# An expert mixer on one Trainium2 core: gathers of four experts for each of 32 tokens, V sums in four column strips, token copies by way of DRAM

## The reference

```python
s = jnp.einsum('nhcd,hckd->nhck', q, keys)
s1, i1 = lax.top_k(s[:, :, 0], PEER_TOPK)
s2, i2 = lax.top_k(s[:, :, 1], PEER_TOPK)
top, sel = lax.top_k(cand, PEER_TOPK)
eidx = jnp.take_along_axis(cidx, sel, axis=-1)
gate = jax.nn.softmax(top, axis=-1)
hid = gelu(jnp.einsum('nkd,nd->nk', U[eb], xb))
out = jnp.einsum('nk,nkd->nd', hid * gb, V[eb])
```

## Time and profile before

| | us |
|---|---|
| median of 3 runs (lowest, highest) | 2206.36 (2205.28, 2214.78) |
| the profiled execution, its own time | 2209.18 |
| its span, first to last instruction | 2207.1 |
| TensorE busy | 2025.8 (92%) |
| VectorE busy | 1443.1 (65%) |
| ScalarE busy | 857.4 (39%) |
| GpSimd busy | 747.4 (34%) |

### The profile page before, as it was taken

The page is one execution under the profiler, slowest core; times in us unless marked ns, Lnnn a source line. Parts: engine busy times, 40 slices in busy tenths (PEclk is TensorE's granted clock), DMA queues, the critical chain, the costliest instruction groups (busy, mean ns, idle before and its releaser), DMA issues.

```text
span 2207.1 us, 37965 instructions
## 1 busy us (share of the span) xinstructions
PE 2025.8 (92%) x13044; PEld 1241.8 (56%) x13044; DVE 1443.1 (65%) x3377; ACT 857.4 (39%) x2476; POOL 747.4 (34%) x658
## 2 busy tenths in 40 slices
PE   7999989999999888999899898899999998789997
PEld 6777668874444223554478776788644442234544
DVE  2425454589999998545442344645999989975555
ACT  2221222144545775433332203221544557753332
POOL 0400000025545676544312000000345557765552
PEclk9999989999999999999999998999999999999999
DMA  6330233678999999999843201437699999999995
GB/s 278 116 116 2 81 112 128 213 254 315 321 352 359 374 354 355 365 379 391 325 187 116 95 8 74 145 134 260 230 325 335 362 370 365 373 380 389 373 383 233
DMA packets 121546, 569.81 MB, mean 258 GB/s; under 512 B 42504, under 2 KB 44712, under 8 KB 61608
## 3 DMA queue, kind: packets, MB, share of 16 engines
q0 software_dynamic: 76032, 389.07, 46.9%
q1 hardware_dynamic: 43648, 175.12, 21.7%
q10 hardware_dynamic: 1696, 3.45, 0.4%
HBM read 725.63 MB, written 6.58 MB: 332 GB/s over the span
## 4 chain that ended last, share of the span: by engine, by line
PE 58%; DVE 21%; issue 10%; DMA 5%; ACT 5%; POOL 1%; another core or an unknown queue 0%; DVEq 0%; SPq 0%; ACTq 0%; POOLq 0%
PE ps L1088 12%; PE ps L1007 11%; PE ps L607 10%; PE ps L672 7%; DVE arena L2091 5%; PE ps L929 3%; PE ps L962 3%; PE ps L943 3%; DMA arena<-in_uv,arena 3%; DMA ring<-in_uv,arena 2%; PE ps L1036 2%; DVE arena L1986 1%; DVE arena L2116 1%; DVE arena L1977 1%; DVE arena L1976 1%
## 5 line engine op out<-in xcount | busy, mean ns | idle before, releaser
L1524 POOL DMA_INDIRECT arena<-in_uv,arena x264 | 342.9, 1299 | 281.3 <-PE ps L1007 229.7
L1524 POOL DMA_INDIRECT ring<-in_uv,arena x264 | 317.8, 1204 | 256.0 <-PE ps L1007 208.6
L2091 DVE SCALAR_TENSOR_TENSOR arena<-arena 128x1024 bf16<-128x1024 f32 x264 | 319.9, 1225 | 118.8 <-DMA arena<-in_uv,arena 113.7
L2091 DVE SCALAR_TENSOR_TENSOR arena<-ring,arena 128x1024 bf16<-128x1024 f32 x264 | 320.3, 1225 | 110.0 <-DMA ring<-in_uv,arena 103.3
L1007 PE MATMUL ps<-arena 64*64 64x512 f32 x2112 | 292.6, 626 | 50.3 <-ACT arena L1416 50.1
L1007 PE MATMUL ps<-ring,arena 64*64 64x512 f32 x2112 | 286.7, 614 | 37.4 <-ACT arena L1416 35.0
L1414 ACT ACTIVATE arena<-arena 128x1 f32<-128x1 f32 x528 | 105.7, 200 | 506.7 <-DVE arena L2091 505.6
L1514 POOL COPY arena<-arena 128x8 uint32 (+1 forms) x66 | 36.4, 552 | 734.9 <-DVEq L2058 734.5
L1088 PEld LDWEIGHTS ps<-hold,ub 128*128 128x128 f32 x1024 | 180.4, 190 | 159.9 <-issue 142.8
L1088 PE MATMUL ps<-hold,ub 128*128 128x256 f32 x1024 | 268.2, 397 | 0.0
L672 PE MATMUL ps<-xn,ring 128*128 128x264 f32 x1024 | 244.5, 398 | 14.3 <-remote 12.2
(11 more groups left out here) (453 smaller groups left out, 2475.9 us busy)
## 6 DMA issues: line engine op xcount, KB each, us to landing
ring<-in_w SPq DMA_DIRECT2D x84, 1024.0 KB, 5.0
ub<-in_uv SPq DMA_DIRECT2D x64, 512.0 KB, 7.7
ub<-in_ud SPq DMA_DIRECT2D x48, 512.0 KB, 7.5
hold<-in_ud SPq DMA_DIRECT2D x16, 512.0 KB, 6.1
ring<-in_uv,arena POOLq DMA_INDIRECT x264, 8.5
arena<-in_uv,arena POOLq DMA_INDIRECT x264, 9.3
ub<-in_w SPq DMA_DIRECT2D x4, 1024.0 KB, 11.0
hold<-in_st SPq DMA_DIRECT2D x2, 2048.0 KB
```

Of the source, the lines that this page charges most:

```text
L1524: e.indirect_dma_start(out=row(k), out_offset=None, in_=A["uv"], in_offset=bass.IndirectOffsetOnAxis(ap=ix[:, par, k:k + 1], axis=0), **sk ...
L2091: stt(prod[:, n % 2, :], u, 1.0, xtok[:, tt, :], ALU.mult, ALU.mult, accum_out=hid[:, k:k + 1]).then_inc(S("dve_hid"), 1)
```

## The change

A gather now serves 32 tokens with four experts each: partition 32 q + t holds expert q of a group's token t. A tile is four groups g; for each two heads (r) and each group there are eight gathers, so their number stays the same. `place(s)` gives tile, r and g of a slot. VectorE multiplies with `rep`, a copy of a group's 32 tokens on all four quarters of the partitions. SyncE makes it: it writes `xtok` to DRAM and reads each group back with the row block named four times (`copies_of_rows`); the reads of the second tile wait until the first tile's last dots of that group are done. The diagonal is 128x32 (`token`), and the sum takes four matmuls over all 128 rows, each with 32 columns of the array and 256 channels of V.

Indices and gates, which routing writes per token, are moved into the new order by ScalarE (`by_tokens`, four copies of 32 partitions for each r and g) into `lay`, and GpSimd waits for these copies (`act_lay`) in place of the routing signal, which comes after the gates. `rep` and `lay` lie over constants that the expert mixer doesn't use; after layer 0 ScalarE loads them again. The first half of the second tile's sum (its groups 0 and 1) is copied, turned and added before the samples' sum is complete, and the second half alone is left for the end. Some loops on TensorE and GpSimd become straight code. Some semaphores are joined (`sp_svw` and `sp_svr`, `dve_yy`, `dve_yc` and `dve_yn`), without another order.

```diff
+TG = 32
+QS = P // TG
...
+    t["group"] = (p[:, None] // 16 == np.arange(TG)[None]).astype(float)
+    t["token"] = (p[:, None] % TG == np.arange(TG)[None]).astype(float)
...
+OVER = CONST_AT["headsum"][0]
...
-        eidx = carve(TT, SLOTS)
-        gate_w = carve(TT, SLOTS)
+        eg = carve(TT, 2, SLOTS)
...
+        rep = const[:, OVER:OVER + QS * D].rearrange("p (a b) -> p a b", b=D)
+        lay = const[:, OVER + QS * D:OVER + QS * D + TT * 2 * SLOTS].rearrange("p (a b) -> p a b", b=2 * SLOTS)
...
-        dg = carve(SLOT, HD)
+        dg = carve(SLOT, TG)
...
+        def place(s):
+
+            tt, n = divmod(s, P)
+            return tt, n // (QS * SLOT), n // SLOT % QS
+
+        def at_place(s):
+
+            tt, r, g = place(s)
+            return (r * QS + g) * 2 * SLOT
...
+                def copies_of_rows(tt):
+
+                    e.wait_ge(S("act_xt"), tt + 1)
+                    e.dma_start(O["scratch_x"][tt * P:tt * P + P, :], xtok[:, tt, :]).then_inc(S("sp_rep"), 16)
+                    for g in range(QS):
+                        if tt:
+                            e.wait_ge(S("dve_hid"), P - (QS - 1 - g) * SLOT)
+                        e.wait_ge(S("sp_rep"), 16 * ((QS + 1) * tt + g + 1))
+                        src = O["scratch_x"][tt * P + g * TG:tt * P + g * TG + TG, :]
+                        e.dma_start(rep[:, g, :], bc(src, 0, [QS, TG, D])).then_inc(S("sp_rep"), 16)
+
...
+                        if j == AHEAD[-1] + 2:
+                            copies_of_rows(0)
...
-                down_blocks(0, 12)
+                down_blocks(0, UB)
+                copies_of_rows(1)
+                down_blocks(UB, 12)
...
-                def weighted(k, tt):
-
+                def weighted(s, b=None):
+
+                    k = s % SLOT
+                    tt, r, g = place(s)
+                    b, lo = (SUM_BANK[tt] + g // 2, D // QS * (g % 2)) if b is None else (b, 0)
                     take(e, dg_full[k], 1)
-                    for half in range(2):
-                        for q in range(2):
-                            m = mm(ps[chunk(q ^ half), SUM_BANK[tt] + half, :], dg[chunk(q), k, :], row(k)[chunk(q), D + 512 * half:D + 512 * half + 512],
-                                   start=False, stop=False, skip_group_check=True)
+                    for q in range(QS):
+                        m = mm(ps[TG * q:TG * q + TG, b, lo:lo + D // QS], dg[:, k, :], row(k)[:, D + D // QS * q:D + D // QS * (q + 1)],
+                               start=False, stop=False, skip_group_check=True)
                     m.then_inc(row_free[k], 1)
...
                     n = SAMPLES_AT * SLOT + P - DOWN_AT + SLOT
                     for s in range(n):
                         if s == n - SLOT:
+                            close_sum(SUM_BANK[1])
                             e.wait_ge(S("dve_xa"), 1)
-                            open_sum(0, 1)
-                        weighted(s % SLOT, 1 if s < n - SLOT else 2)
+                            open_sum(0)
+                        if s == n - SLOT // 2:
+                            turned(1, 0, 3)
+                        weighted(DOWN_AT + s, None if s < n - SLOT else SUM_BANK[2])
...
-                with e.Fori(0, 2) as i:
-                    up_slots(2)
+                up_slots(2)
...
-                close_sum(2)
+                close_sum(SUM_BANK[2])
                 for k in range(SLOT):
-                    weighted(k, 1)
+                    weighted(P + SAMPLES_AT * SLOT + k)
                     if k == 7:
                         sum_squares_first(l)
                     if k == 3:
                         e.wait_ge(S("act_acc"), 4)
-                        for kt in range(KT):
-                            from_ = NS // 2 * (kt // 4)
-                            m = mm(bank(0, NS, NS * kt), xtok[:, 2, kt * P:kt * P + P], C("group")[:, from_:from_ + NS], start=True, stop=True)
+                        for half in range(2):
+                            m = e.transpose(bank(0, P, P * half), xtok[:, 2, P * half:P * half + P], C("ident"))
                         m.then_inc(S("pe_xa"), 1)
-                close_sum(1)
-                for half in range(2):
-                    turned(1, half, 5 + half)
+                close_sum(SUM_BANK[1] + 1)
+                turned(1, 1, 5)
...
+                def by_tokens(n, g):
+
+                    if g == 0:
+                        e.wait_ge(S("dve_route"), n)
+                    tt, r = divmod(n - 1, GROUPS)
+                    to = lay[:, tt, (r * QS + g) * 2 * SLOT:(r * QS + g + 1) * 2 * SLOT].rearrange("p (a k) -> p a k", a=2)
+                    for q in range(QS):
+                        of = r * QS * SLOT + q * SLOT
+                        i = act(to[q * TG:q * TG + TG], eg[g * TG:g * TG + TG, tt, :, of:of + SLOT], ACT.Copy)
+                    i.then_inc(S("act_lay"), 1)
...
                     if o == KT - 2:
                         exponentials()
+                        by_tokens(1, 0)
...
+                for g in range(1, QS):
+                    by_tokens(1, g)
+
+                def gelu(k, n, gate, of="token"):
 
                     e.wait_ge(S("dve_hid"), n + 1)
                     own(act(hge[:, k:k + 1], hid[:, k:k + 1], ACT.Gelu))
                     own(act(hgg[:, k:k + 1], hge[:, k:k + 1], ACT.Copy, scale=gate))
-                    act(dg[:, k, :], C("channel"), ACT.Copy, scale=hgg[:, k:k + 1]).then_inc(dg_full[k], 1)
-
-                def sums_out(tt, nth):
+                    act(dg[:, k, :], C(of), ACT.Copy, scale=hgg[:, k:k + 1]).then_inc(dg_full[k], 1)
+
+                def sums_out(tt, nth, half, n=512):
                     e.wait_ge(S("pe_acc"), nth)
-                    for half in range(2):
-                        act(xtok[:, tt, 512 * half:512 * half + 512], bank(SUM_BANK[tt] + half, 512), ACT.Copy).then_inc(S("act_acc"), 1)
+                    act(xtok[:, tt, 512 * half:512 * half + n], bank(SUM_BANK[tt] + half, n), ACT.Copy).then_inc(S("act_acc"), 1)
...
+                moved = {SECOND_AT[2] + 2 + g: (2, g) for g in range(QS)}
+                moved |= {ROUTE_FROM + ROUTE_EVERY * (r - 2) + PIECES[5] + 2 + g: (r + 1, g) for r in range(2, 2 * GROUPS) for g in range(QS)}
                 e.wait_ge(S("sp_out"), 5 * 16)
...
+                    if s == 0:
+                        e.wait_ge(S("act_lay"), QS)
                     if s == samples:
                         own.clear()
                         for k in range(SLOT):
-                            gelu(k, s + k, gs[:, k:k + 1])
+                            gelu(k, s + k, gs[:, k:k + 1], "group")
+                        sums_out(1, 2, 0)
...
+                    if s in moved:
+                        by_tokens(*moved[s])
+                        e.wait_ge(S("act_lay"), QS * (moved[s][0] - 1) + moved[s][1] + 1)
...
-                        sums_out(0, 1)
-                    tt, n = divmod(s, P)
-                    gelu(s % SLOT, s + (SLOT if s >= samples else 0), gate_w[:, tt, n:n + 1])
+                        for half in range(2):
+                            sums_out(0, 1, half)
+                    at = at_place(s) + SLOT + s % SLOT
+                    gelu(s % SLOT, s + (SLOT if s >= samples else 0), lay[:, s // P, at:at + 1])
                     if s == samples + 2:
-                        sums_out(2, 2)
-                sums_out(1, 3)
+                        sums_out(2, 3, 0, D // QS)
+                if l + 1 < L:
+                    e.dma_start(const[:, OVER:NCONST], A["const"][:, OVER:NCONST]).then_inc(S("act_const"), 16)
+                sums_out(1, 4, 1)
...
-                for tt in range(TT):
-                    for g in range(GROUPS):
-                        e.wait_ge(S("dve_route"), ROUTED[tt][g])
-                        with e.Fori(0, PER_GROUP // 2 - (tt == 1 and g == GROUPS - 1)) as i:
-                            own.clear()
-                            for par in range(2):
-                                indices(par, eidx[:, tt, bass.ds(i * 16 + g * GH * TOPK + SLOT * par, SLOT)].bitcast(U32))
-                                fetch(par, tt == g == par == 0, **in_range)
+                for s in range(0, TT * P, SLOT):
+                    tt, r, g = place(s)
+                    if s == SAMPLES_AT * SLOT + P:
+                        e.wait_ge(S("sp_sr"), 64)
                         own.clear()
-                for par, n in ((0, SAMPLES_AT - 1), (1, None), (0, SAMPLES_AT)):
-                    if n is None:
-                        e.wait_ge(S("sp_sr"), 64)
-                        indices(par, es)
-                        fetch(par)
-                    else:
-                        indices(par, eidx[:, 1, n * SLOT:n * SLOT + SLOT].bitcast(U32))
-                        fetch(par, **in_range)
+                        indices(1, es)
+                        fetch(1)
+                    par = 0 if s == SAMPLES_AT * SLOT + P else g % 2
```

(54 more changed lines are left out.)

72 lines of the change are left out of this document (36 added, 36 removed).

## The result

The changed kernel takes **2340.0 us** (2335.8 to 2355.9, 4 runs) where the kernel before takes 2208.6 (4 runs beside it): a ratio of 1.0608, 95% interval 1.0579 to 1.0636. I had forecast 2194, and a range up to 2236. The profiled execution took 2339.7 us, its span 2337.9, 130.8 more than the span of before.

What follows compares the result with a forecast made beforehand. VectorE was taken to bound slots 0 to 167, TensorE the last stage with the DMA next. Terms -27 + 18 - 8 + 2 + 3 = -12 us gave a median of 2194 us, range 2162 to 2236.

Steps and rivals of the forecast that it cites:

- V sums: Last stage of both layers: a set falls from 1.09 to 0.65 us, the DMA gives way, -27 us.
- TensorE under 90%: Sign that the forecast is right: TensorE busy under 90% in the last stage, with that stage over 405 GB/s.
- I take 410: Last stages: the DMA rate was assumed to rise from 382 and 386 to 410 GB/s, giving -15 and -12 us.
- rival C: Last stages: the DMA is full, its rate stays at 382 to 386 GB/s, no gain from V sums, 2221 us; chance 0.12.
- Token copies at the first dot: Start of each layer's mixer: the first dot waits for tokens written to DRAM and read back, +9 a layer, +18 us.
- The bound from above: First dot of a layer: at most 14 us late, with 7.7, 8.6 and 4 more for a read on fewer engines.
- Token copies in slots 0 to 167: The copies' DMA load beside the gathers, half in slots 96 to 167: 1 us a layer taken from 0 to 7.
- Rival B: The four-fold read runs on four DMA engines and delays gathers, mostly slots 104 to 135: 21 us a layer, 2236 us; chance 0.18.
- Waits that go: Slots 0 to 167: VectorE's waits for rows (4.9 us) and L1365 (6.3 us) shrink, 4 a layer, -8 us.
- End of a layer: After the last gather: -2 from shorter final steps, +3 from turning tile 1's first half early; +1 a layer, +2 us.
- Indices and gates by ScalarE: Slots 7 to 95: 128 small copies a layer, 24 us of ScalarE, hidden, and no delay to the first gather.

Runs made afterwards that it cites:

- run 1: The changed kernel with each of the 16 token reads split into four DMAs, one per quarter of the partitions, outermost count 32 in place of 4: 2277.9 us.
- run 2: The changed kernel with the token copies read straight from SBUF, four DMAs of 32 partitions each, without the write to DRAM: 2269.9 us.
- run 6: The changed kernel with copies straight from SBUF, but only the first of a layer's eight made, so other groups' dots use wrong rows: 2225.8 us.
- run 11: The changed kernel with token copies made by ScalarE, and tile 1's first half turned one stage later: 2236.1 us, against 2245.2 without the later turn.
- run 8: The kernel before with the right 256 of each 512 columns of its V sums left out, nothing else of the change: 2193.1 us.
- run 12: The kernel before with only 128 of each 512 columns of its V sums made, nothing else of the change: 2182.2 us.
- run 4: The kernel before with the V sums' matmuls of the lower 64 rows left out, half of them: 2329.6 us.
- run 7: The kernel before with the V sums' matmuls that write the second bank left out, half of them: 2215.4 us.

## Why the prediction was wrong

Step by step the loss comes apart as 62 us for reads with an outermost count of 4 in place of 32 (run 1), 8 for the trip to DRAM (run 2), 44 for the copies themselves (run 6), and 16 that run 6 is above the kernel before, of which some 9 are the early turn of tile 1's sums (run 11). By the prediction's own terms, both layers together:

- **V sums, -27: measured +4.** The price of a set was right (0.64 us for 0.65), and so was TensorE under 90%. The step that failed is "I take 410": the DMA stays at 381 and 386 GB/s. Alone (run 8) the cheaper sums reach 391, so rival C, the DMA is full, was right but for 4 to 5 us a layer. I took 410 from 80 us at 400 and single slices of up to 434 GB/s; these show what the engines do for some microseconds, and no last stage of any run held more than 397 (run 8, layer 1).
- **Token copies at the first dot, +18: measured +29** (11.3 and 17.9 more after the first gather), and 7.5 from later first gathers, which I had put at nothing and which differ by up to 10 us from run to run (454 to 464 us in layer 1). The bound from above, 14 a layer, had 12.6 us for a read (8.6 and 4 more); it takes 18.
- **Token copies in slots 0 to 167, +2: measured +84.** This is the step that made the sign wrong: "Of between 0 and 7 us a layer I take 1". It rested on the 410, by which there would be room at a share of 0.96. The runs show none: with an outermost count of 32 the copies still cost 44 us (runs 2 and 6), and with 4 they cost 62 more (run 1).
- **Rival B** was right about the outermost count of 4, which cost the other 62 us (run 1), and I gave it 0.18. That four engines moved such a read was its assumption; the traces show only that no more than 4 to 6 packets of a read in tile 1 were under way at a time. Its price was 21 us a layer, 31 were measured. It counted only the read's own packets on four engines, 3.6 us net a read; slots 96 to 167 lost 4 to 5 us a read. I also added this price to a forecast whose other terms were wrong, so that B came to 2236 us, the end of the range, where 2340 was measured. Its test, VectorE waiting over 10 us for rows in slots 104 to 135, came true: 25 us.
- **Waits that go, -8: next to nothing.** The waits for rows grew, and the wait at L1365's line still takes 4.5 us in each layer (6.3 before).
- **End of a layer, +2: measured +6**, by the wait for ScalarE that I named; by run 11 it is 4.6 us a layer and not 3.
- **Indices and gates by ScalarE, nothing: nearly right.** Run 6 has them all, and its slots 0 to 95 take 239 us for 235 in layer 0; 2.5 of these 4 us are VectorE's wait at L1365's line (8.8 us for 6.3). TensorE waits for no dense block in any of these stages, so the loads behind the copies on SyncE's queue cost nothing, as I said.
- **The clock** is in none of my terms. It falls to 0.69 in slots 96 to 167, where TensorE is busy 103 of 183 us. Here that cost nothing that shows (run 6: 148 us at 0.76; run 12, with still cheaper sums: 147 at 0.60): a set of the new form at half the clock is as long as one of the old form at full clock, 1.08 us (at 784 us, where the granted clock is 0.50) and 1.09, and TensorE stays idle for a third of run 6's stage. Run 4 shows what the clock costs where TensorE is the bound.

```profile
784.28 1.08 PE L1039 MATMUL ps<-arena 128*32 128x256 f32 x8 [2.80 <-ACT arena L1463]
```

What stays open: run 6 is 33 us slower than run 8, which has V sums of the same price and none of the rest. Some 9 us are that turn; of the others 7 to 8 lie in layer 0's last stage, 218 us at 377 GB/s against 210 at 391, and why the new gathers are slower there no run tells. Nor does one tell why the copies of runs 2 and 6 cost twice the time of their bytes.

## What to carry to other kernels

Before a step is made cheaper, find the next bound and price it over the whole stage: here a DMA at 0.99 gave 4 us of a hoped-for 15, and the copies added for the sake of the cheaper step cost 44 us beside a DMA at a share of 0.96. Look at the outermost count of each DMA's access pattern: with 4 in place of 32, sixteen reads of 512 KB cost 62 us beside gathers, whose longest landing rose from 15.8 to 23.3 us. When an engine is relieved, ask what its clock will do, and whether anything waits for it then: TensorE's fell from 1.00 to 0.69 in slots 96 to 167, and nothing that shows hung on it; at 0.55 in run 4 the same slots took 43 us more.

## What was not expected of the hardware

Runs 4 and 7 issue the same number of matmuls of the same size, two of 64x64 by 512 columns a set. With both in the same 64 rows the granted clock was 0.55 in slots 96 to 167, with the two in different rows and columns 1.00; TensorE was busy 98% of the time in the first and 80% in the second. A full engine at a clock of 0.55 I had not expected.

The DMA held 391 and 396 GB/s over 210 us (runs 8 and 12), at shares of 0.99 and 1.00, where the kernel before moved 382 GB/s in the same stage at a share of 0.99 already.
